# A new order of the ScalarE and VectorE work inside each step of a dilated-attention stage

## The reference

```
GROUPS = ((128, 1), (512, 4), (2048, 16))        # (window, dilation), 16 heads of 64 each
qkv = (x @ w_in).reshape(b, s, 3, N_GROUPS, HEADS, 64)
for g, (window, dilation) in enumerate(GROUPS):
    q = rms_norm(qkv[:, :, 0, g], q_gain[g]) * 64 ** -0.5
    k = rms_norm(qkv[:, :, 1, g], k_gain[g])
    o, l = dilated_window_attention(q, k, qkv[:, :, 2, g], rel_bias[:, g], window, dilation)
wts = softmax(stack(lses), axis=0)                # merge the three groups
y = einsum('gbsh,gbshe->bshe', wts, stack(outs)) @ w_out
```

## Time and profile before

| | before |
|---|---|
| median of 3 runs | 3298.39 us |
| profiled execution, its own time | 3298.39 us |
| span of that execution | 3296.7 us |
| PE busy | 3122.4 us (95%) |
| DVE busy | 1307.0 us (40%) |
| ACT busy | 1099.3 us (33%) |
| POOL busy | 925.5 us (28%) |

### The profile page before, as it was taken

The page is one execution under the profiler, slowest core; times in us unless marked ns, Lnnn a source line. Parts: engine busy times, 40 slices in busy tenths (PEclk is TensorE's granted clock), DMA queues, the critical chain, the costliest instruction groups (busy, mean ns, idle before and its releaser), DMA issues. The chain is left out here.

```text
span 3296.7 us, 44438 instructions
## 1 busy us (share of the span) xinstructions
PE 3122.4 (95%) x16122; PEld 2694.2 (82%) x16122; DVE 1307.0 (40%) x3533; ACT 1099.3 (33%) x3146; POOL 925.5 (28%) x790
## 2 busy tenths in 40 slices
PE   4999999999999995999999999899777999999999
PEld 3999999999999974788888888778566788888887
DVE  6446555555645554431313133520164422313131
ACT  4555555555555552211111113111253211111110
POOL 3444444444444421222222222222202222222221
PEclk7999999999999987999999999999898999999999
DMA  3223222222323214111111111111211111111112
GB/s 105 59 63 85 66 80 74 74 78 69 84 62 83 68 32 173 45 45 52 51 45 52 45 52 46 39 45 45 77 39 52 45 45 51 46 50 52 45 52 77
DMA packets 143125, 201.85 MB, mean 61 GB/s; under 512 B 29611, under 2 KB 109118, under 8 KB 142910
## 3 DMA queue, kind: packets, MB, share of 16 engines
q1 hardware_dynamic: 140606, 194.81, 19.2%
q10 hardware_dynamic: 2304, 4.20, 0.3%
HBM read 173.25 MB, written 25.70 MB: 60 GB/s over the span
## 5 line engine op out<-in xcount | busy, mean ns | idle before, releaser
L69 PE MATMUL ps_qk<-w_hi,attn_hT_hi 128*128 128x384 f32 x1536 | 538.0, 350 | 16.0 <-DVE attn_hT_lo L213 9.7
L71 PE MATMUL ps_qk<-w_hi,attn_hT_lo 128*128 128x384 f32 x1536 | 517.1, 337 | 0.0
L70 PE MATMUL ps_qk<-w_lo,attn_hT_hi 128*128 128x384 f32 x1536 | 516.8, 336 | 0.0
L989 POOL TENSOR_TENSOR first_w_lo<-first_raw,first_w_hi 128x1024 fp32r<-128x1024 f32 x96 | 231.6, 2413 | 852.6 <-ACT first_w_hi L985 852.6
L989 POOL TENSOR_TENSOR second_w_lo<-second_raw,second_w_hi 128x1024 fp32r<-128x1024 f32 x72 | 173.3, 2407 | 620.4 <-ACT second_w_hi L985 620.4
L69 PEld LDWEIGHTS ps_qk<-w_hi,attn_hT_hi 128*128 128x128 f32 x1536 | 289.7, 189 | 38.6 <-DVE attn_hT_lo L213 11.6
L70 PEld LDWEIGHTS ps_qk<-w_lo,attn_hT_hi 128*128 128x128 f32 x1536 | 290.5, 189 | 0.0
L71 PEld LDWEIGHTS ps_qk<-w_hi,attn_hT_lo 128*128 128x128 f32 x1536 | 290.2, 189 | 0.0
L69 PE MATMUL first_ps<-first_hid_hi,first_w_hi 128*128 128x512 f32 x640 | 250.7, 392 | 32.0 <-DVE first_hid_lo L1315 32.0
L953 POOL TENSOR_TENSOR rs<-var,minus_half 128x4 f32<-128x4 f32 x192 | 193.5, 1008 | 303.5 <-DVE var L813 303.3
L69 PE MATMUL first_ps<-first_hT_hi,first_w_hi 128*128 128x512 f32 x640 | 251.8, 393 | 14.2 <-POOL first_w_lo L989 14.2
(11 more groups left out here) (267 smaller groups left out, 6153.5 us busy)
## 6 DMA issues: line engine op xcount, KB each, us to landing
raw<-in_wqkv SPq DMA_DIRECT2D x192, 192.0 KB, 2.4
first_raw<-in_w SPq DMA_DIRECT2D x64, 512.0 KB, 3.2
second_raw<-in_w SPq DMA_DIRECT2D x64, 512.0 KB, 3.2
v_dram<-ring SPq DMA_DIRECT2D x192, 64.0 KB, 1.5
w_bc<-share_dram SPq DMA_DIRECT2D x48, 256.0 KB, 4.5
v_raw<-v_dram SPq DMA_DIRECT2D x32, 256.0 KB, 3.1
first_raw<-in_vo_pieces SPq DMA_DIRECT2D x16, 512.0 KB, 3.3
bias<-bias_dram SPq DMA_DIRECT2D x16, 256.0 KB, 3.4
```

The costliest lines, as they stand in the source:

```text
L69: pe.matmul(out, a_hi, b_hi, start=first, stop=False)
L70: pe.matmul(out, a_hi, b_lo, start=False, stop=False)
L71: return pe.matmul(out, a_lo, b_hi, start=False, stop=last)
L989: pool.tensor_tensor(self.lo[:, n % 2, :], self.raw[:, n % self.RAW, :], self.hi[:, n % 2, :].bitcast(F32), ALU.subtract).then_inc(self.lo ...
```

## The change

In steps of superstep 1 and later the pieces of ACT and DVE stand in another order. PE, POOL and SP keep theirs, and no instruction is added or taken away.

```
@@ scalar engine @@
-                weights()
                 exponentials()
+                turned_tiles()
+                outputs()
                 unit_values()
                 if j == 3 and st >= 4 and (st - 4) % NG == 0:
                     act.wait_ge(diff_done, (st - 4) // NG + 1)
                     act.activation(grown[:], diff[:], ACT.Exp).then_inc(grown_done, 1)
-                if j == 0:
-                    turned_tiles()
-                    squares_and_values()
-                else:
-                    squares_and_values()
-                    turned_tiles()
-                outputs()
+                weights()
+                squares_and_values()
                 turned_probabilities()
@@ vector engine @@
                 maxima()
+                turned_tiles()
                 merge_step(st, j)
-                if j == 0:
-                    turned_tiles()
-                    variances()
-                else:
-                    variances()
-                    turned_tiles()
+                variances()
+                turned_probabilities()
                 normalise()
-                turned_probabilities()
```

## The result

The changed kernel takes 3408.07 us (median of 4 runs, 3404.45 to 3408.97) against 3297.84 us, a ratio of 1.0334 (95% interval 1.0316 to 1.0351): slower by 110 us, where 107 were forecast. Its profiled execution took 3402.49 us with a span of 3400.8 us.

What follows compares the result with a forecast made beforehand. PE's own pace bounded the kernel; the change would make a longer ring through ACT, POOL and DVE set it. 67 (ring) + 2 (j = 0) + 38 (merges) = 107 us on 3298.39 gave 3405 us, range 3345 to 3475.

Steps and rivals of the forecast that it cites:

- The ring: ACT's exponentials to w_hi, POOL's w_lo, v_lo, rs, DVE's qkn, maxima, next exponentials: 6.68 us wide, 6.20 narrow.
- The way by the squares and `var`: From exponentials over ACT's squares and DVE's var to POOL's rs: 2.75 us, shorter than POOL's 3.27.
- j = 0 and 1: Only j = 0 was forecast: PE's scores also wait for qk_lo, about 0.3 us in eight narrow cases, 2 us.
- The merges: DVE's merge operations, now between qk_lo and the reduction, delay rs and stop w_lo: 38 us, within 16 to 41.
- the small chain: DVE's 1.92 us of small merge operations: +1.5 us at the upper bound, 0.6 at the lower.
- The covers: Later pT_lo, w_lo for a section's last weight tile, v's way out and back, next weight load: cost nothing.
- PE's wait: Sign: PE waits for ACT's prob at ps_p in nearly every step, 80 us or more in total.
- No change: Rival: the new order costs nothing because POOL hands on faster than its rows say; 3298 us, chance 0.06.
- faster: Rival: the turned tile copied first removes PE's waits for qk_hi and around the scores; about 3287 us, chance 0.05.
- The merges at the lower bound: Rival: the ring is there, but DVE's merges cost only 16 us; 3383 us, chance 0.22.
- The clock: Rival: PE's stops drop its clock to 1.2 GHz in 18 steps, adding 100 us; about 3505 us, chance 0.07.
- PEclk stays at 1.00: Sign that the forecast is right: PE's granted clock keeps at 1.00, that is 2.4 GHz.

Runs made afterwards that it cites:

- rs_first: The changed kernel with POOL's order rs, w_lo, v_lo in place of w_lo, v_lo, rs: 3361.24 us, ratio 1.0198.
- weights_first: The changed kernel with ScalarE's w_hi back at the front of the step: 3322.72 us, ratio 1.0081.
- twice_after: The changed kernel with POOL making every w_lo of supersteps 0 to 22 twice, the second waiting for the first: 3598.39 us, ratio 1.0913.
- merge_back: The changed kernel with merge_step back ahead of turned_tiles on VectorE: 3375.36 us, ratio 1.0238.
- twice_before: The kernel before the change with every w_lo made twice on POOL, the second waiting for the first: 3297.40 us, ratio 0.9998.
- both_back: The changed kernel with w_hi back at the front of the step on ScalarE and merge_step back ahead of turned_tiles on VectorE: 3302.78 us, ratio 1.0015.
- dve_only: The kernel before the change with only VectorE's pieces in the new order, ScalarE's in the old: 3350.64 us, ratio 1.0163.
- act_only: The kernel before the change with only ScalarE's pieces in the new order, VectorE's in the old: 3452.86 us, ratio 1.0477.
- norm_first: The changed kernel with normalise back ahead of turned_probabilities on VectorE: 3492.77 us, ratio 1.0593.

## Why the prediction was right

- **The ring as the new bound.** Right, and through the engines that were named: rs_first, weights_first and twice_after each change one member of it and move the time by it. Forecast 6.68 and 6.20 us a step, measured 6.64 and 6.16. The way by the squares and `var`, forecast at 2.75 us against 3.27 by POOL, is 2.91 (rs_first) against 3.23: still the shorter one. The sum of supersteps 1 to 22 without anything else was forecast as 67 us. By the measured steps it is 60: 8 x 3.04 + 7 x 2.39 + 7 x 2.71. The prediction set 49.12 us for every superstep of group 0, but superstep 1 took 47.57 before; that is 1.5 us more.
- **j = 0 and 1.** The term that was mis-sized: 2 us forecast, about 15 measured (merge_back's 76.2 less the 60 and 1.5 of superstep 1). In merge_back, in the 15 supersteps in which PE also transposes `stat`, the step j = 1 is 6.87 us and not 6.16. PE comes out of step 0 late, because its scores waited for `qk_lo`, then has one transpose more, and ACT waits some 0.4 us for it ahead of the turned tile. I had seen the first part and missed that the second comes on top. How the 0.71 us divide between the two was not tested. The rest are small operations in supersteps that begin a merge (6.56 at j = 1, 6.81 at j = 3).
- **The merges.** Forecast 38 us of 16 to 41, measured 34.5, or 31 without the four falls of the clock. Against merge_back the steps with a 2.02 us multiplication are 1.22 and 1.25 us longer (forecast 1.75 and 1.3), those with a 1.22 us one 0.41 (0.5), the small chain 0.83 (1.5). Superstep 23 had been taken as free and came out 2.5 us longer, by its merges. The stop of `w_lo` is seen in its rows. How much of the 34.5 is the stop and how much the later `var` no run separates cleanly. In rs_first, where `w_lo` does not stand ahead of `rs`, a step with a 1.22 us multiplication is 0.10 us longer than its neighbours and not 0.41, which points to 0.3 us for each stop by such a one. The Trainium skill's rule (SBUF — State Buffer, Who interferes with whom), that GpSimd stands still to the end of such a VectorE instruction, agrees with 2.23 against 1.01 us.
- **The covers.** `pT_lo`, the last weight tile and v's way out and back cost nothing that shows: PE's new waits are for `prob`, with 4.8 us for `qkn`, 12 times.
- **PE's wait.** Forecast 80 us or more at `ps_p`, in nearly every step. The matmul rows show 57.8 us in 115 steps, the weight-load rows 90.5 in 143, and PE's idle time rose by 69.
- **The rivals.** No change and faster are out. The merges at the lower bound are out (34.5 against 16). The clock did fall, so the sign "PEclk stays at 1.00" failed, but in four places, for some 3.5 us in all (below), not in 18 steps.
- **What was luck.** The mechanism and the ring were right, the closeness of the total less so. Forecast were 67, 2 and 38 us, measured 61.5, 15 and 34.5; the errors of -5.5, +13 and -3.5 nearly cancel, to 110.75 against 107.

## What to carry to other kernels

Where engines are half busy and yet one of them waits, write down the ring: follow one step's result through every queue until it releases the same instruction of the next step, add the distances, and compare with the step of the engine that is full. An instruction in that ring costs its whole time, and one with enough room beside it nothing. Taken out of the ring, it gives back only the difference to the next longest way round: rs_first gave back 47 us, weights_first 85. A moved instruction takes what waits for it on another engine, and all that is queued behind that, into the ring with it. Doubling one instruction (twice_after, twice_before) tells in one run whether it is in the ring.

## What the runs showed of the hardware that was not expected

**Tiny operations of VectorE are stopped by GpSimd too.** `neg_max` (128x2) took 0.41 us beside `v_lo` in rs_first and 0.17 us elsewhere, and `var` (128x4) took 0.55 us beside the delayed `w_lo` in the changed kernel and 0.17 before. Both ended within 0.03 us of the POOL instruction. The prediction had only looked for the stop in the other direction.

**The clock fell after some of the long merge steps.** The granted clock of the changed kernel in stretches of 2 us of superstep 8:

```profile
478.00:480.00 2.00, 1.48 (x9) 0.92 (x7) 1.39 (x7) 0.03 (x1) 0.49 (x1) 1.00 0.48 131
480.00:482.00 2.00, 0.95 (x6) 0.62 (x6) 0.46 (x2) 1.96 (x9) 0.00 (x0) 0.84 0.00 0
482.00:484.00 2.00, 2.00 (x10) 1.88 (x11) 1.97 (x4) 1.68 (x5) 1.27 (x1) 0.50 0.00 0
484.00:486.00 2.00, 2.00 (x12) 2.00 (x11) 1.20 (x5) 0.00 (x0) 1.54 (x3) 0.81 0.38 89
```

PE ahead of the fall, with its stops in brackets:

```profile
479.09 0.41 PE L564 MATMUL ps_t<-ident,qkn 128*128 128x128 f32 x2 [0.47 <-DVE qkn L826]
...
481.05 0.88 PE L602 MATMUL ps_p<-ident,prob 128*128 128x128 f32 x4 [1.10 <-ACT prob L663]
```

PE had stood still for 0.47 us and, 0.86 us after it had gone on, for 1.10 us. In supersteps 8, 11, 17 and 20 the clock went to 0.50, that is 1.2 GHz, and in the next step ACT waited 0.75 to 0.79 us for PE's transposes: 8.25 to 8.30 us for that step in place of 7.40. The same two stops did not always do it. In supersteps 5 and 14 they were 0.45 and 1.12 us and 0.46 and 1.13 us, and the clock stayed at 1.00, 2.4 GHz. Nor did it fall at the second long multiplication of any superstep, where PE stood still for up to 1.14 us after a shorter stop. What tips it was not found.

The other traces show the same in the stretch: no fall in the kernel before, merge_back, weights_first, rs_first, twice_before and both_back, four in dve_only, five in act_only, 14 in norm_first and 26 in twice_after, the two slowest kernels. The falls do not follow the loss alone: dve_only, 52 us longer in the stretch, has four and merge_back, 76 us longer, none.
